# A two-block model kernel: one step for each level of RWKV's triangular inverse with another order of the steps beside it, and the last three tiles cut into 320 and 192 tokens

## The reference

```python
def wkv7_scan(r, w, k, v, a, b):
    def step(state, inp):
        r_t, w_t, k_t, v_t, a_t, b_t = inp
        sa = jnp.einsum('bhvk,bhk->bhv', state, a_t)
        state = (state * w_t[:, :, None, :]
                 + sa[..., None] * b_t[:, :, None, :]
                 + v_t[..., None] * k_t[:, :, None, :])
        y_t = jnp.einsum('bhvk,bhk->bhv', state, r_t)
        return state, y_t
...
        h3 = rmsnorm_2(x, ln3[i])
        x = x + jax.nn.sigmoid(h3 @ w_pg[i]) * (p[i] @ w_pp[i])
    return rmsnorm_2(x, ln_f)
```

## Time and profile before

| | us |
|---|---|
| median of 3 runs (1943.46 to 1946.0) | 1943.49 |
| the profiled execution, its own time | 1944.14 |
| its span, first to last instruction | 1942.0 |
| PE busy in the span | 1912.8 (98%) |
| DVE busy | 983.5 (51%) |
| ACT busy | 777.3 (40%) |

### The profile page before, as it was taken

How to read it: one execution, slowest core, us unless ns; L and a number is a source line. 1 busy time by engine, 2 the same in 40 slices (tenths; PEclk the granted TensorE clock), 3 DMA queues, 4 the chain that set the end, 5 groups by cost and what they waited for, 6 DMA issues and landing times.

```text
span 1942.0 us, 27868 instructions
## 1 busy us (share of the span) xinstructions
PE 1912.8 (98%) x11648; PEld 1566.1 (81%) x11648; DVE 983.5 (51%) x1550; ACT 777.3 (40%) x1260; POOL 291.6 (15%) x286
## 2 busy tenths in 40 slices
PE   8999999999999999999999999999999999999997
PEld 6877777778888888888788888888888888888886
DVE  6666666656432333367745344459444432333365
ACT  6665233254443332345433333354233433232345
POOL 2001323302210010122000000015110311010124
PEclk9999999999999999999999999999999999999999
DMA  5222111145233323233322222222322342223221
GB/s 201 66 87 76 62 51 56 62 140 172 95 106 122 111 89 103 91 109 125 114 66 70 72 81 82 87 76 87 108 95 81 112 137 98 98 98 98 97 87 55
DMA packets 60080, 185.71 MB, mean 96 GB/s; under 512 B 6595, under 2 KB 11843, under 8 KB 59828
## 3 DMA queue, kind: packets, MB, share of 16 engines
q1 hardware_dynamic: 59956, 183.94, 28.5%
HBM read 173.69 MB, written 10.22 MB: 95 GB/s over the span
## 4 chain that ended last, share of the span: by engine, by line
PE 88%; DVE 5%; ACT 2%; issue 2%; POOL 1%; DMA 1%; SPq 0%; DVEq 0%; POOLq 0%; ACTq 0%
PE P L578 26%; PE P L580 25%; PE P L579 25%; DVE AREN L1771 2%; DVE AREN L1774 1%; POOL AREN L2516 1%; ACT WHI L1177 1%; PE P L1109 1%; DVE WLO L1778 1%; PE P L914 1%; PE P L926 1%; PE P L930 1%; PE P L767 0%; POOL AREN L2519 0%; PE P L1060 0%
## 5 line engine op out<-in xcount | busy, mean ns | idle before, releaser
L578 PE MATMUL P<-HH,WHI 128*128 128x512 f32 x1528 | 613.1, 401 | 6.2 <-DVE HL L1791 3.6
L580 PE MATMUL P<-HH,WLO 128*128 128x512 f32 x1528 | 596.3, 390 | 0.0
L579 PE MATMUL P<-HL,WHI 128*128 128x512 f32 x1528 | 595.6, 390 | 0.0
L1177 ACT ACTIVATE WHI<-RAW 128x1024 fp32r<-128x1024 f32 x302 | 318.0, 1053 | 419.6 <-PE P L580 418.8
L1778 DVE TENSOR_TENSOR WLO<-RAW,WHI 128x1024 fp32r<-128x1024 f32 x302 | 375.9, 1245 | 144.7 <-ACT WHI L1177 143.2
L578 PE MATMUL P<-ARR,WHI 128*128 128x512 f32 (+1 forms) x920 | 353.1, 384 | 0.0
L579 PE MATMUL P<-ARR,WHI 128*128 128x512 f32 (+1 forms) x920 | 352.9, 384 | 0.0
L580 PE MATMUL P<-ARR,WLO 128*128 128x512 f32 (+1 forms) x920 | 352.8, 384 | 0.0
L578 PEld LDWEIGHTS P<-HH,WHI 128*128 128x128 f32 x1528 | 286.8, 188 | 76.3 <-issue 6.7
L580 PEld LDWEIGHTS P<-HH,WLO 128*128 128x128 f32 x1528 | 286.8, 188 | 61.5
L579 PEld LDWEIGHTS P<-HL,WHI 128*128 128x128 f32 x1528 | 287.2, 188 | 56.3 <-issue 1.0
(11 more groups left out here) (313 smaller groups left out, 1424.5 us busy)
## 6 DMA issues: line engine op xcount, KB each, us to landing
RAW<-in_w_in_dram SPq DMA_DIRECT2D x117, 512.0 KB, 3.3
RAW<-in_w_ff_dram SPq DMA_DIRECT2D x64, 512.0 KB, 3.3
RAW<-in_w_ml_dram SPq DMA_DIRECT2D x64, 512.0 KB, 3.3
RAW<-in_w_out_dram SPq DMA_DIRECT2D x16, 512.0 KB, 3.3
RAW<-in_w_pg_dram SPq DMA_DIRECT2D x16, 512.0 KB, 3.3
AREN<-in_xT_dram SPq DMA_DIRECT2D x16, 256.0 KB, 5.7
s_gates<-AREN SPq DMA_DIRECT2D x16, 256.0 KB, 2.0
RAW<-in_w_ab_dram SPq DMA_DIRECT2D x8, 512.0 KB, 3.3
```

The source lines that it names most:

```text
L578: e.matmul(out, hi, H[0][:, s], start=first, stop=False)
L579: e.matmul(out, hi, H[1][:, s], start=False, stop=False)
L580: return e.matmul(out, lo, H[0][:, s], start=False, stop=last)
L1177: e.activation(WHI[n % NSPL][:, :], RAW[n % NRAW][:, :], ACT.Copy).then_inc(*D.act.sig("whi", n))
```

## The change

- `core_steps`: a level is one step V. For lev 1 to 5 it forms both products of the two matrices X and Q (16 matmuls for a pair group); DVE multiplies the one by the level's mask, which now holds the identity too (Y), and copies the other (S). V 6 holds what was in the last `lb`. Step S is gone; its state product stands at the head of O, N's matmuls stand in M, and the state product of `second` in N. T's matmuls stand behind G's, in banks 6 and 7, and `mean` waits until DVE has read them.
- There are 51 steps for 70, spread by a number of rows each, not evenly.
- `front`'s DVE work is regrouped; its four steps stand at V3, V6, M and N instead of la 3, lb 4, W and N.
- POOL makes the starting matrix of a quarter in two additions a pair group (before: four multiplications and an addition).
- The x tiles are loaded one every four rows, from the 31st row of the merge stage, no longer between the gates.
- The last three tiles run on 320 and then 192 tokens. The first part's total comes behind row 2 of the second part's tile 6, its root, its results and their stores ahead of the second part's elementwise steps. For that ACT loads the other table set and back.

```diff
+
+PARTS = (slice(0, 320), slice(320, 512))
+
+
 def last_steps(j, k):
 
+
     at = {(0, 7): "evac", (1, 0): "sigmoid", (1, 1): "mult", (1, 2): "add", (1, 3): "square", (1, 4): "sum"}
-    return [(5 + u % 3, u // 3, at[j - 5 - u, k]) for u in range(6) if (j - 5 - u, k) in at]
+    late = {(0, 7): "evac", (1, 5): "sigmoid", (1, 6): "mult", (1, 7): "add", (2, 0): "square", (2, 1): "sum"}
+    steps = [late if u == 3 else at for u in range(6)]
+    return [(5 + u % 3, u // 3, steps[u][j - 5 - u, k]) for u in range(6) if (j - 5 - u, k) in steps[u]]
...
-        out += [("G", q, 0), ("T", q, 0)]
-        for lev in range(1, 6):
-            out += [("la", q, lev), ("lb", q, lev)]
-        out += [("W", q, 0), ("M", q, 0), ("N", q, 0)] + ([("S", q, 0)] if q < 3 else []) + [("O", q, 0)]
-    return out + [("E", 3, i) for i in range(3)]
+        out += [("G", q, 0, 27), ("T", q, 0, 25)]
+        out += [("V", q, lev, (22, 22, 26, 28, 24, 25)[lev - 1]) for lev in range(1, 7)]
+        out += [("W", q, 0, 25), ("M", q, 0, 25), ("N", q, 0, 22), ("O", q, 0, 25)]
+    return out + [("E", 3, i, 20) for i in range(3)]
...
-    seq = []
-    for what, q, lev in core_steps():
-        seq.append(["c", "e"] + (["f"] if q < 3 and (what in "WN" or (what, lev) in (("la", 3), ("lb", 4))) else []))
-    n = len(seq)
-    for i, group in enumerate(seq):
-        put_steps(at, A_GA + i * 125 // n, group)
+    steps, r = core_steps(), 0
+    n = sum(s[3] for s in steps)
+    for what, q, lev, rows in steps:
+        group = ["c", "e"] + (["f"] if q < 3 and (what in "MN" or (what, lev) in (("V", 3), ("V", 6))) else [])
+        put_steps(at, A_GA + r * 125 // n, group)
+        r += rows
...
-                    cs = slice(256 * half, 256 * half + 256)
+                    cs = PARTS[half]
                     for t, b in zip((5, 6, 7), banks):
                         w.wait_ge(D.dve.at("wlo", T_PG2 + t), free.get(b))
                         for k in range(8):
-                            d = row(bank(b)[:, 0:256], T_PG2 + t, k, (H3[k][0][:, cs], H3[k][1][:, cs]), k == 0, k == 7)
...
                                 d.then_inc(*D.pe.sig("pg2", t, half))
-                                if half and t == 6:
-                                    last_total(0, 7)
+                            if (t, half, k) == (6, 1, 2):
+                                last_total(0, 7)
                             yield
                 last_total(1, 0)
...
-                    o = take(b, C.act.at("y", q))
+                    o = take(b, C.act.at("y", q), CO[0].dve.at("t", min(q + 1, 3), 1))
...
-                    if what == "la":
-                        o = [take(b, C.dve.at("T", q, lev - 1)) for b in (b0, b1)]
...
-                    if what == "lb":
...
+                    if what == "V" and lev < 6:
+
+                        marks = (C.dve.at("Y", q, 0), C.pool.at("S0", q)) if lev == 1 else (C.dve.at("S", q, lev - 1),)
+                        o = [v3(take(b, *marks)[:, 0:256], 2) for b in (b0, b1)]
+                        for i in range(2):
+                            for j, p, h in jhp:
+                                at, to = rws[p ^ (h & (lev - 1))], rws[p ^ (h & lev)]
+                                a, x = v3(Qm, 4)[at, 2 * j + h, :], v3(Xm, 4)[at, 2 * j + h, :]
+                                d = e.matmul(o[h][to, j, 64 * i:64 * i + 64], *((a, x), (x, a))[i], start=True, stop=True)
+                        d.then_inc(*C.pe.sig("v", q, lev))
...
                             free[(b0, b1)[p]] = C.dve.at("QT", q, p)
-                    if what == "N":
-                        o = take(b0, C.act.at("U", q, 1))
+                        o = take(bw, C.act.at("U", q, 1))
                         for j, p, h in jhp:
                             d = e.matmul(kj(o[:, 0:256], j, p, h), BT[:, j, p, 64 * h:64 * h + 64],
                                          VU[:, j, p, 64 * h:64 * h + 64], start=True, stop=True)
                         d.then_inc(*C.pe.sig("n", q))
-                        free[b0] = C.act.at("N", q)
-                    if what == "S":
-                        state(2 * q + 1, b0)
+                        free[bw] = C.act.at("N", q)
...
+                    if (j, k) == (9, 4):
+                        last_rs(0, 7)
...
-                    if t == 7 and half:
+                    if t == 7:
                         e.preload_act_table_set("natural_log_exp_and_others")
...
+                    if (j, k) == (9, 5):
+                        result(0, 2, 5)
...
-                result(0, 2, 8)
+                result(0, 5, 8)
...
                     mul(v2["kk"], Kq, col("k_k")).then_inc(*F.dve.sig("kk", q))
+                    yield
+                    w.wait_ge(F.pe.at("ss", q))
+                    e.tensor_scalar(tmp, bank(6 + jj)[:, 0:256], 1e-24, None, op0=ALU.max).then_inc(
+                        *F.dve.sig("max", q))
                     w.wait_ge(F.pool.at("rk", q - 1))
                     e.scalar_tensor_tensor(out=v2["kp"], in0=Aq, scalar=-1.0, in1=col("k_a"), op0=ALU.add,
                                            op1=ALU.mult).then_inc(*F.dve.sig("ka", q))
@@ -2222,11 +2225,7 @@
                     e.scalar_tensor_tensor(out=v2["kp"], in0=v2["kp"], scalar=1.0, in1=Kq, op0=ALU.add,
                                            op1=ALU.mult).then_inc(*F.dve.sig("kp", q))
                     yield
-                    w.wait_ge(F.pe.at("ss", q))
-                    e.tensor_scalar(tmp, bank(6 + jj)[:, 0:256], 1e-24, None, op0=ALU.max).then_inc(
-                        *F.dve.sig("max", q))
-                    yield
-                    w.wait_ge(C.pe.at("t", q - 1, 1), F.pool.at("bh", q - 1, 1), F.dve.at("kp", q))
...
-                    if what == "la":
-                        w.wait_ge(C.pe.at("la", q, lev), C.dve.at("st", 2 * q) if lev == 1 and q else None)
-                        mul(hj(Xm), both(b0, 64, 64), lb4(lev)).then_inc(*C.dve.sig("X", q, lev))
-                    if what == "lb":
-                        w.wait_ge(C.pe.at("lc", q, lev), C.pool.at("Q", q))
-                        if lev < 5:
-                            add(hj(Tm), hj(Tm), both(b0, 64, 64)).then_inc(*C.dve.sig("T", q, lev))
-                        else:
-                            add(Qm, Qm, o0[:, 0:256]).then_inc(*C.dve.sig("Q", q, 5))
+                    if what == "V" and lev < 6:
+                        w.wait_ge(C.pe.at("v", q, lev))
+                        mul(hj(Xm), both(b0, 128, 128)[:, :, :, 0:64], lb4(lev)).then_inc(*C.dve.sig("Y", q, lev))
+                        e.tensor_copy(hj(Qm), both(b0, 128, 64)).then_inc(*C.dve.sig("S", q, lev))
...
-                            for h in range(2):
-                                w.wait_ge(C.dve.at("gm", q, h), C.pe.at("w", q - 1), C.pool.at("q0", q, p, 0) if h else C.pool.at("q0", q, 0, 1) if p else None)
-                                mul(p_.Qm_h[rws[p ^ h], :, h, :], p_.Gv[rws[p], h, :, p, 0, :],
...
+                            w.wait_ge(C.dve.at("gm", q, 1), C.pe.at("w", q - 1), C.pool.at("s0", q) if p else None)
+                            add(hj(p_.Qm)[rws[p]], p_.Gv[rws[p], :, :, p, 0, :],
+                                cst("i64")[rws[p]].unsqueeze(1).unsqueeze(1).to_broadcast([64, 2, 2, 64])).then_inc(
+                                *C.pool.sig("S0" if p else "s0", q))
...
+                    if i % 4 == 2 and 30 <= i < 62:
+                        x = (i - 30) // 4
+                        load(f"x{x}", 1, ar(XB + x), A["xT"][:, T * x:T * (x + 1)])
...
-                load(f"x{j}", 1, ar(XB + j), A["xT"][:, T * j:T * (j + 1)])
```

More of the change, by code:

```diff
@@ L847, in second @@
                 def second(what, q, lev):
-                    if what == "la":
+                    if what == "T" and q:
+                        mean(q - 1, bw)
+                    if what == "V":
                         if lev == 1:
-                            o = take(bw, *[cc(8 + 2 * jj + j) for j in range(2)])
+                            o = take(bw, CO[0].dve.at("t", q, 1), *[cc(8 + 2 * jj + j) for j in range(2)])
                             for j in range(2):
@@ L884, in second @@
                         free[b1] = C.act.at("y", q)
[L886 removed]
+                for what, q, lev, _ in core_steps():
                     _, _, Vq, _, _, _ = p_.q(q)
@@ new lines, in core @@
+                        o = [v3(take(6 + h)[:, 128 * jj:128 * jj + 128], 2) for h in range(2)]
+                        for j, p in jp4:
+                            for h in range(2):
+                                d = e.matmul(o[h][rws[p], j, :], AR[rws[h], j, 0, p, :], BK[rws[h], j, 3 * p, :],
+                                             start=True, stop=True)
+                        d.then_inc(*C.pe.sig("t", q))
+                        if jj == 1:
+                            free[6] = free[7] = C.dve.at("t", q, 1)
@@ new lines, in core @@
+                    if what == "V" and lev == 6:
```

(24 more changed lines are left out.)

148 lines of the change are left out of this document (56 added, 92 removed).

## The result

The changed kernel takes 1919.91 us (median; 1919.36 to 1920.06), the kernel before beside it 1943.73 (1943.46 to 1946.0). The ratio is 0.9874, interval 0.9862 to 0.9887: 1.3% faster. The forecast was 1926.0, 6 us too slow. The profiled execution took 1920.06 us, 24.1 less than that of before (1944.14).

The account below looks back on a forecast made before the run. PE, busy 98% of the span, was taken as the bound, except at the end. From 1944.14 us, -9.2 - 3.8 - 3.0 - 1.5 + 0.0 = -17.5 gave 1926.6, or 1926.0 against the median; whole range 1919.5 to 1934.

Parts of the forecast that it names:

- Records on PE: RWKV stage: 20 V steps at 28.8 to 31.0 us replace `la` and `lb` steps of 39.2; 9.2 us saved.
- Rival 4: Levels don't get shorter: V's crosswise products run one behind the other; 1953.6 us, slower; chance 0.03.
- Rival 2: PE finds almost no wait and V runs at 22.5 ns a record or less: 1920.9 us; chance 0.07.
- Seams: Changes between small blocks and dense rows on PE: 20 fewer at 0.19 us each, 3.8 us saved, bounds 2.2 to 4.2.
- Waits in the stage: PE's idle time in the RWKV stage falls from 7.25 to 4.3 us: 3.0 gained, bounds gain 6 to loss 3.
- `mean`'s new one: In step T `mean` waits until DVE has read T for both groups: 1.6 us over three quarters.
- Gates: PE's 2.0 us wait for WLO shrinks once x tiles leave that transfer burst: 1.5 us gained, bounds 0.3 and 2.0.
- The end: Last tiles in 320 and 192 tokens: last total 4.4 us late, shorter stores after it; 0.0 gained, bounds -2 and +2.
- Rival 3: A drain behind the two table loads on the chain that ends last: 1927.4 to 1928.8 us; chance 0.04.

Follow-up runs that it names:

- v_same: The changed kernel with V's matmuls reordered so that four in a row use the same row half and column half of the array: 1949.61 us.
- x_only: The kernel before with the later loads of x alone: 1942.52 us beside 1943.92, ratio 0.999.
- end_only: The kernel before with the changed end alone (320 and 192 tokens, early root and its stores): 1943.9 us, ratio 1.0001.

## Why the forecast was 6 us too high

- **Records on PE: wrong, 15.2 us instead of 9.2.** The step that failed: "V has the regular order of `la` and writes two banks as `lb`, so I take the middle". That fewer steps with cheaper records on PE make most of the gain was right, the price of V's records was not. It was carried over from `la` and `lb` as if it were a constant. It hangs on where the matmuls land: `lb` was bound by its 12 matmuls on each of two quadrants, V spreads 8 on each of four; a V step took 1.09 us where the sum had 1.49. The forecast also took `la`'s price at a step behind a wait, 0.72 where a step that didn't wait takes 0.62; that made the old levels 2 us too dear and hid part of the error (20 x (1.49 - 1.09) = 8.0 too much for V, 2.2 too much for what was removed, the balance 6). One lone `la` of 0.62, 19.4 ns a record, would have warned that V can be cheaper than 22.5. That the miss was no larger was also luck: the clock's drop, which the forecast didn't have, took 1.6 us of the gain back in the profiled execution.
- **Rival 4 named the right question with the wrong answer.** It feared that crosswise products run one behind the other. They run beside the direct ones; with four in a row on one quadrant (v_same) the kernel is indeed slower than before, 1.0025 (1.0016 to 1.0035). Rival 2 had V at 22.5 ns or less and 1920.9: it came nearest, though its other half, hardly any wait, did not come true.
- **Seams: 3.8 forecast, 3.4 shown.** A seam is 0.21 us, not 0.19, but only the 16 in the levels were saved. By the same reading, from the dense matmul ahead to the second one behind less 0.46, G and T cost 2.18 + 0.87 before and 3.17 as one block; M, N, the two state steps and O 6.98 before and 6.96 now. Folding those together gave nothing: the time of such a block is its matmuls.
- **Waits in the stage: 3.0 forecast, 2.3 measured** (7.25 idle to 4.97). The waits of 3.6 and 2.0 us in the levels went, as forecast. From the stage's first dense row on (183.4 to 412.8 before, 183.5 to 391.5 now) the idle time is 8.6 and 5.8, 2.8 less. `mean`'s new one is 4.5 and not 1.6, because DVE's queue has a dense tile's evacuation ahead of T's masks and that waits for PE; I had counted DVE's work there without what DVE itself waits for.
- **The clock: nothing forecast, 1.6 lost.** The forecast priced `mean`'s wait by its length alone. Behind the longest one the granted clock was 0.50, and that cost three quarters as much again as the wait.
- **Gates: 1.5 forecast, 2.0 in the profile**, 1.4 in x_only. Right, as was its cause.
- **The end: 0.0 forecast, 0.2 measured**, and nothing in end_only. The loads of tables cost what the row had said, the second part's late start was taken back by shorter stores. Rival 3, a drain, did not happen.
- The sum, with the whole stage's idle time, is 15.2 + 3.4 + 2.8 + 2.0 + 0.2 - 1.6 = 22.0 of 24.1 us. Steps around waits took longer than the prices above even without their idle time: the 20 `la` 13.5 us for 12.4, the 16 `lb` 24.8 for 24.6, the 20 V 22.2 for 21.8; that is 0.9 more. The last 1.2 us stay open.

## What to carry to other kernels

Price small matmuls by where they land, not by their number: count how many of a block fall on each row half and column half, and expect the fullest quadrant to set the time; then order them so that no long row falls on one or two quadrants. Spreading work evenly (V against `lb`) gave 0.45 us of 1.54; reordering an evenly loaded block (M) gave 0.28 of 0.90; reordering an unevenly loaded one (`lb`, V 6) gave nothing. Take a duration from a row that had not just waited, and when a wait on an in-order engine is estimated, look at what the engine's own queue waits for. A wait of PE can cost more than its length: behind 2.1 us the clock dropped in three of eight profiled executions, and where I priced it, that took 1.6 us more.
